# Layer-1 products started on half of the modulation, and its query and key products cut into 256-column matmuls

## The reference, cut to what matters

```
mod = silu(c) @ w_ada + b_ada                 # w_ada: 2048 x 6144, 50 MB
shift, scale, gate = split(mod, 3)
h = rms_norm(x, norm_gain) * (1 + scale) + shift
proj = h @ w_in                               # w_in: 2048 x 8192, 67 MB
q_sb, k_sb, v_sb, z_sb, q_r, k_r, v_r, z_r = split(proj, 8)
... stick-breaking attention on (q_sb, k_sb, v_sb), gated by silu(z_sb)
... chunkwise retention on (q_r, k_r, v_r), gated by silu(z_r)
x = x + gate * (concat(oa, ob) @ w_out)
```

## Time and profile before

| what | value |
|---|---|
| runs shown | 1885.12 us median of 3 (1883.63 to 1887.93) |
| the profiled execution, its own time | 1890.45 us |
| its span, first to last instruction | 1888.6 us |
| TensorE busy, share of the span | 94% |
| VectorE, ScalarE, GpSimd | 65%, 48%, 4% |
| moved from HBM | 346.87 MB |
| mean granted TensorE clock | 0.976 of full speed |

### The profile page before, as it was taken

The page is one execution under the profiler, slowest core; times in us unless marked ns, Lnnn a source line. Parts: engine busy times, 40 slices in busy tenths (PEclk is TensorE's granted clock), DMA queues, the critical chain, the costliest instruction groups (busy, mean ns, idle before and its releaser), DMA issues.

```text
span 1888.6 us, 23572 instructions
## 1 busy us (share of the span) xinstructions
PE 1784.2 (94%) x9703; PEld 1517.6 (80%) x9703; DVE 1235.9 (65%) x1520; ACT 902.7 (48%) x1158; POOL 75.7 (4%) x87
## 2 busy tenths in 40 slices
PE   1699999999999989999999999999989999999897
PEld 1577888888887878888888888788878888878786
DVE  3978767655477655788567766865464667566754
ACT  2333544454356434666344565644354555455632
POOL 0111000000000000011000000000000000000010
PEclk9798999999999999999999999999989999999999
DMA  8897888556444546666654555565546565444463
GB/s 304 328 350 294 296 290 298 153 148 177 135 145 141 190 149 169 188 189 180 178 145 138 153 167 162 167 191 185 187 141 178 162 194 146 123 123 123 134 187 115
DMA packets 304874, 350.51 MB, mean 186 GB/s; under 512 B 10416, under 2 KB 286000, under 8 KB 298624
## 3 DMA queue, kind: packets, MB, share of 16 engines
q1 hardware_dynamic: 297744, 298.34, 52.5%
q0 software_dynamic: 7024, 50.66, 6.9%
HBM read 346.87 MB, written 2.10 MB: 185 GB/s over the span
## 4 chain that ended last, share of the span: by engine, by line
PE 90%; DVE 5%; DMA 2%; ACT 2%; issue 2%; SPq 0%; DVEq 0%
PE psG L431 48%; PE psG L432 24%; PE psG L425 3%; PE psG L426 3%; PE psG L427 3%; DVE ada_sum L1062 1%; DMA P<-in_memT 1%; PE psH L1615 1%; DMA raw<-in_mem_w 1%; PE psH L1604 1%; DVE w_lo L368 1%; PE psH L1629 1%; DVE W L1003 1%; ACT w_hi L364 1%; PE psH L1890 1%
## 5 line engine op out<-in xcount | busy, mean ns | idle before, releaser
L431 PE MATMUL psG<-xA,w_hi 128*128 128x512 f32 x3520 | 1281.8, 407 | 53.4 <-issue 24.4
L432 PE MATMUL psG<-xA,w_lo 128*128 128x256 f32 x3520 | 994.7, 283 | 0.0
L368 DVE TENSOR_TENSOR w_lo<-raw,w_hi 128x1024 fp32r<-128x1024 f32 (+1 forms) x560 | 686.5, 1239 | 356.9 <-ACT w_hi L364 355.4
L431 PEld LDWEIGHTS psG<-xA,w_hi 128*128 128x128 f32 x3520 | 670.0, 190 | 226.5 <-issue 50.1
L364 ACT ACTIVATE w_hi<-raw 128x1024 fp32r<-128x1024 f32 (+1 forms) x560 | 572.9, 1045 | 372.2 <-DMA raw<-in_w_out 163.9
L432 PEld LDWEIGHTS psG<-xA,w_lo 128*128 128x128 f32 x3520 | 673.7, 191 | 4.4 <-issue 3.8
L400 ACT ACTIVATE P<-psG 128x512 f32<-128x512 f32 x102 | 60.6, 594 | 217.5 <-PE psG L432 217.4
L1033 DVE TENSOR_TENSOR P<-psG,P 128x512 f32<-128x512 f32 (+2 forms) x103 | 70.4, 683 | 116.4 <-ACT P L400 114.1
L1062 DVE SCALAR_TENSOR_TENSOR ada_sum<-ada_ring,silc,ada_sum 128x2048 f32<-128x2048 f32 x48 | 112.6, 2347 | 3.9 <-DMA ada_ring<-in_w_ada 3.8
L425 PE MATMUL psG<-w_hi,xA 128*128 128x512 f32 x192 | 77.7, 405 | 4.4 <-DVE memkv L1033 3.9
L426 PE MATMUL psG<-w_lo,xA 128*128 128x512 f32 x192 | 76.9, 400 | 0.0
(11 more groups left out here) (291 smaller groups left out, 1492.0 us busy)
## 6 DMA issues: line engine op xcount, KB each, us to landing
raw<-in_w_in SPq DMA_DIRECT2D x360, 512.0 KB, 3.8
raw<-in_w_out SPq DMA_DIRECT2D x128, 512.0 KB, 3.4
ada_ring<-in_w_ada POOLq DMA_DIRECT2D x48, 1024.0 KB, 7.9
raw<-in_mem_w SPq DMA_DIRECT2D x32, 512.0 KB, 9.3
raw<-in_w_uq SPq DMA_DIRECT2D x24, 384.0 KB, 3.3
raw<-in_w_ukv SPq DMA_DIRECT2D x32, 128.0 KB, 2.4
raw<-in_w_ukv SPq DMA_DIRECT2D x16, 256.0 KB, 3.2
P<-in_memT SPq DMA_DIRECT2D x1, 2048.0 KB, 25.6
```

What stands on the lines that cost most here:

```text
L368: nc.vector.tensor_tensor(slot(w_lo, n), slot(raw, n), slot(w_hi, n), ALU.subtract).then_inc(lo_ready, 1)
L431: nc.tensor.matmul(psG[:, bank + f, :], hi[:, w], x, start=first, stop=False)
L432: last = nc.tensor.matmul(psG[:, bank + f, S:2 * S], lo[:, w], x[:, 0:S], start=False, stop=end)
```

## The change

It has three parts (1 to 3), and a fourth that they bring with them.

1. Modulation in two column halves. The order of `w_ada` is now: columns 0 to 1023 of shift and scale (32 loads of 512 KB), then columns 1024 to 2047 of both (32 loads). The ring has six buffers of 512 KB. The first half is added during `G_MEM` (one per unit, two in each of the first four), then half of the columns of the modulation are summed, and eight of the 16 tiles of the norm are made, in the hooks of the last three units. GpSimd issues its first `w_ada` load after it has helped with the memory's sum of squares (`add_squares(0)`, new), and stops at the 21st for `add_squares(1)`.
2. Layer-1 products split along the rows. `G_SBQK0`, `G_RTQK0`, `G_SBV0` (16, 16 and 8 units) multiply the rows 0 to 1023 of their weights by the tiles of the first half, and ScalarE copies the result to SBUF. During them the second half of the modulation is added, and the other eight tiles are made in the last three units. `G_SBQK`, `G_SBV`, `G_RTQK` (16, 8 and 16 units now) do the rows 1024 to 2047, and VectorE adds their result from PSUM. A block of the four query and key products now has two units instead of four. Half of the `sb_hook` work moves to `G_RTV`.
3. These four query and key products use three matmuls of 256 columns per block of weights (high by high, high by low, low by high) into one half of a bank, so that one engine alone takes the result.
4. The 16 gate loads of 1 MB by GpSimd become 32 of 512 KB that SP issues into the same six `raw` slots as the weights, one after every second weight chunk in `G_SBQK`, `G_SBV`, `G_RTV`, `G_SBZ`, one after every fourth in `G_RTQK` (`GATE_AT`). A slot with a gate chunk is free again when VectorE has added it. The memory is loaded in four pieces ahead of the constants, `x` after the first eight weight chunks.

```diff
-ADA_SLOTS = 4
-ADA_FIRST, ADA_BLOCK = 8, 6
+ADA_SUM, ADA_RING, GATE_SUM = 64, (48, 52, 56, 60, 72, 76), 60
+ADA_HALF = 32
+MEM_UNITS, EARLY_UNITS = 32, 40
...
+        G_SBQK0, G_SBQK = (Gemm(8, 8, columns(w_in, 0, row0=k0 * NP), dst=into(SBQ), pair=True, **early(k0), **one_half) for k0 in (0, 8))
+        G_RTQK0, G_RTQK = (Gemm(8, 8, columns(w_in, 4096, row0=k0 * NP), dst=into(RTQ), **early(k0), **one_half) for k0 in (0, 8))
+        G_SBV0, G_SBV = (Gemm(8, 2, columns(w_in, 2048, 512, 2, row0=k0 * NP), cols=512, kk=2, tokens=copy_tokens(SBV),
+                              **early(k0)) for k0 in (0, 8))
...
+        ORDER = [*G_MEM, G_SBQK0, G_RTQK0, G_SBV0, G_SBQK, G_SBV, G_RTQK, G_RTV, G_SBZ, G_RTZ, G_OUT,
...
+        GATE_AT = {G_SBQK: lambda i: i % 2 == 1, G_SBV: lambda i: i % 2 == 1, G_RTQK: lambda i: i % 4 == 3,
+                   G_RTV: lambda i: i % 2 == 1, G_SBZ: lambda i: i % 2 == 1}
+        ITEMS = []
+        for g in ORDER:
+            for i in range(len(g.order)):
+                ITEMS.append(("weight", g.c0 + i))
+                if g in GATE_AT and GATE_AT[g](i):
+                    ITEMS.append(("gate", sum(kind == "gate" for kind, _ in ITEMS)))
...
+            for j in range(j, end):
+                kind, n = ITEMS[j]
+                if j >= SLOTS:
+                    before, m = ITEMS[j - SLOTS]
+                    sp.wait_ge(*((chunk_used, m + 1) if before == "weight" else (ada_used, 2 * ADA_HALF + m + 1)))
+                if kind == "gate":
+                    k, half = m_to_gate(n)
+                    sp.dma_start(raw[:, j % SLOTS, :], ada_rows(k, 2, half)).then_inc(raw_loaded[j % SLOTS], 16)
+                    continue
...
+                            if g.halves == 1:
+                                out = psG[:, bank + f, 0:S]
+                                nc.tensor.matmul(out, hi[:, w], x[:, 0:S], start=first, stop=False)
+                                nc.tensor.matmul(out, hi[:, w], x[:, S:2 * S], start=False, stop=False)
+                                last = nc.tensor.matmul(out, lo[:, w], x[:, 0:S], start=False, stop=end)
+                                continue
...
             sp.dma_start(vec[:, :], io["vec"]).then_inc(loaded["vec"], 16)
+            for g in range(4):
+                sp.dma_start(mem_raw[:, 4 * g:4 * g + 4, :], io["memT"].rearrange("(t p) s -> p t s", p=NP)[:, 4 * g:4 * g + 4, :])\
+                  .then_inc(mem_loaded[g], 16)
             sp.dma_start(con[:, :], io["con"]).then_inc(loaded["con"], 16)
...
                 load_weights(sp, g)
+                if g is G_MEM[0]:
+                    sp.dma_start(xT[:, :, :], io["xT"].rearrange("(t p) s -> p t s", p=NP)).then_inc(loaded["x"], 16)
...
+            add_squares(0)
+            for m, (half, k, part) in enumerate(ADA_ORDER):
+                slot = m % len(ADA_RING)
+                if m == 20:
+                    add_squares(1)
+                if m >= len(ADA_RING):
+                    pool.wait_ge(ada_used, m + 1 - len(ADA_RING))
+                pool.dma_start(ada_ring[slot][:, :], ada_rows(k, part, half)).then_inc(ada_loaded[slot], 16)
...
+            def gate_hook(g, u0=0):
+                def hook(b, p):
+                    i = 8 * b + p // 2
+                    if p % 2 and GATE_AT[g](i):
+                        ada_add(2 * ADA_HALF + ITEMS[PLACE["weight", g.c0 + i] + 1][1])
+                return hook
...
+            run(G_SBQK, gate_hook(G_SBQK))
+            run(G_SBV, gate_hook(G_SBV))
...
             run_products(pe, G_RTQK, sb_hook)
-            run_products(pe, G_RTV)
+            pe.wait_ge(q["sb_y"], 2)
+            gate_columns(0)
+            run_products(pe, G_RTV, lambda b, p: sb_hook(2 + b, p))
             pe.wait_ge(q["sb_y"], 4)
-            pe.wait_ge(ada_used, 3 * KT)
-            ada_columns(1, 2 * KT, "gate_cols")
...
             run_products(pe, G_SBZ, rt_hook)
+            pe.wait_ge(q["rt_y"], 2)
+            gate_columns(1)
             run_products(pe, G_RTZ, lambda b, p: rt_hook(2 + b, p))
```

More of the change, by code:

```diff
@@ L268, in build, with early @@
         h1 = dict(x=from_a, ready=norm_ready(1))
+        def early(k0):
+            return dict(x=lambda k: xA[:, k0 + k, :], ready=lambda tiles: (q["nm_lo"], 16 + k0 + tiles), adds=k0 > 0, per=8)
+        one_half = dict(halves=1)
         w_in, mem_w = io["w_in"], io["mem_w"]
@@ L445, in build @@
         sb_v, rt_v = (tiles(t, 8).rearrange("p (h f) -> p h f", h=2) for t in (SBV, RTV))
[L446 to L447 removed]
+        ADA_ORDER = [(half, k, part) for half in range(2) for k in range(KT) for part in range(2)]
         GATED1 = [(SBQ, SBZ), (SBQ + 4, SBZ + 4), (RTQ, RTZ), (RTQ + 4, RTZ + 4)]
@@ L679, in _ @@
             run(G_RTQK, sb_hook)
-            run(G_RTV)
             act.wait_ge(loaded["con1"], 16)
+            run(G_RTV, lambda b, p: sb_hook(2 + b, p))
             def rt_hook(n, p):
@@ new lines, in half_norm, with ada_units @@
+            def half_norm(half, step):
+                if step == 0:
+                    modulation(half)
+                    dve.wait_ge(q["nm_rs"], 2)
+                for t in (range(0, 4), range(4, 7), range(7, 10))[step]:
+                    norm_step(1, xT, gs, mod, 8 * half + t, 8 * half, 8 * half + 8)
+            def ada_units(units):
+                done = [0]
+                for u in range(units):
+                    done.append(done[-1] + (u < units - 4) + (units == MEM_UNITS and u < 4) - (units == EARLY_UNITS and u % 9 == 8))
+                return done
@@ new lines, in ada_hook @@
+            def ada_hook(u0, units, half):
+                done = ada_units(units)
+                def hook(b, p):
+                    if p % 2 == 0:
+                        u = u0 + 8 * b + p // 2
+                        for m in range(done[u], done[u + 1]):
+                            ada_add(ADA_HALF * half + m)
+                        if u >= units - 3:
+                            half_norm(half, u - (units - 3))
+                return hook
+            for i, g in enumerate(G_MEM):
+                run(g, ada_hook(8 * i, MEM_UNITS, 0), hook_first=False)
@@ L1142, in sb_hook, with both, hook @@
                     v.tensor_scalar(tiles(n * 2 + SBQ, 2), psH[:, BB, :], 1.0, None, ALU.mult).then_inc(q["sb_y"], 1)
-            run(G_RTQK, sb_hook)
-            run(G_RTV)
-            dve.wait_ge(q["gate_cols"], 1)
-            link(v.tensor_tensor(mod[:, 32:48], psH[:, BD, 32:48], V("b_ada", 32, 16), ALU.add))
+            def both(*hooks):
+                def hook(b, p):
+                    for h in hooks:
+                        h(b, p)
+                return hook
+            run(G_RTQK, both(sb_hook, gate_hook(G_RTQK)))
+            gate_columns(0)
+            run(G_RTV, both(lambda b, p: sb_hook(2 + b, p), gate_hook(G_RTV)))
             sin2 = C1("sin", S).unsqueeze(1).broadcast_to([NP, 2, S])
@@ L1200, in z1_hook @@
                     gate_1(n - 1)
-            run(G_SBZ, z1_hook)
+            run(G_SBZ, both(z1_hook, gate_hook(G_SBZ)))
+            gate_columns(1)
             run(G_RTZ, lambda b, p: z1_hook(2 + b, p))
@@ L1624, in sums_hook, with ada_columns @@
                 return hook
-            def ada_columns(part, column, name, first=True, last=True):
-                for t in range(KT):
-                    ins = mm(psH[:, BD, column + t:column + t + 1], ada_sum[:, part, t * NP:t * NP + NP],
-                             ones[:, 0:1], start=first and t == 0, stop=last and t == KT - 1)
-                ins.then_inc(q[name], 1)
+            def ada_columns(src, column, name, first=True):
+                for t in range(8):
+                    ins = mm(psH[:, BD, column + t:column + t + 1], src[:, t * NP:t * NP + NP], ones[:, 0:1],
+                             start=first and t == 0, stop=bool(name) and t == 7)
+                if name:
+                    ins.then_inc(q[name], 1)
```

342 lines of the change are left out of this document (185 added, 157 removed).

## The result

The changed kernel takes 1969.13 us (median; 1960.5 to 1972.39), the kernel before 1886.53 beside it: a ratio of 1.0428, interval 1.0386 to 1.0471. That is 83 us slower where 8 were forecast, and outside the range of 1852 to 1925. The profiled execution's span is 1970.5 us.

What follows compares the result with a forecast made beforehand. TensorE, busy 94% of 1888.6 us, was taken as the bound. Terms before the gates summed to -47, gates +55, together +8: 1893 us against the median of 1885.12; 8-in-10 range 1852 to 1925, the forecast's own 1880 to 1912.

Steps and rivals of the forecast that it cites:

- Three matmuls of 256 columns: Layer's query and key products: 512 pairs become triples at 0.350 us for 0.353; 0 to -1.5 us, taken as 0.
- Start-up: Before the first product: root at 18.5 us instead of 38.1, first product at 27.8; -21.8 us (-15 to -24).
- The units of `G_MEM`: The 32 units of the memory stage take 106.3 us for 127.9; -21.6 us.
- up to the old pace: Early half-units after `G_MEM`: 10.2 us of serial norm go, 3.7 for columns and 3 for 40 units charged; -3.5 us.
- The cost of `x` in one load: In `G_MEM`: `x` queued behind the eighth chunk makes the ninth come late; +5 us (0 to 10).
- The gate chunks: From `G_SBQK` to `G_RTZ`: gate loads in the weights' slots make TensorE wait for weights; +55 us (30 to 76).
- SP's order closes a circle: Gate stages: addition frees a slot, but waits behind the split of a weight queued behind that slot; 8.2 us per two units.
- the circle's landing: Link in the gate stages' cycle: a load lands in 3.4 us plus 0.8 behind the gate chunk's own data.
- one gate in four units: In `G_RTQK`: gates this far apart close no such cycle; +2 us.
- a clock that drops in the gaps: Gate stages: TensorE's lower clock in its pauses is mostly absorbed by them; no size given.
- the first: Rival, gate stages: cycle hidden, landing near 3.4 us, lead never used up; 1868 or 1838 us; chances 0.20 and 0.13.
- The early part bound by DMA: Second rival, through the early units: 76 MB to load, 20 us of the gain lost, 1913 us; chance 0.12.

Runs made afterwards that it cites:

- a4_pairs: Changed kernel with the layer's queries and keys again by a 512-column and a 256-column product into a whole bank, row split kept; 1968.1 us.
- a1_no_gates: Changed kernel without gate chunk loads, their additions and the gate's column sums, the gate being its bias alone; 1852.7 us, 0.9814 of the kernel before.
- a3_small_gates: Changed kernel with each gate load cut to 32 of 1024 columns, additions, slots, waits and order unchanged; 1944.6 us, 1.0319 of the kernel before.
- a2_add_first: Changed kernel with VectorE's gate addition ahead of its unit's split instead of behind it; 1906.0 us, 1.0107 of the kernel before.
- d1_empty_slots: Changed kernel without gate loads, additions and column sums, but each gate chunk's slot kept empty for its turn; 1891.0 us, 1.0008 of the kernel before.
- b3_both: Changed kernel with gate chunks on GpSimd's queue into three own buffers and two sums, additions moved, and xT in four pieces; 1853.6 us, 0.9821 of the kernel before.

## Why the prediction was wrong

**Three matmuls of 256 columns: right.** Twelve matmuls in the changed kernel's timeline, a weight load for each:

```profile
395.73 0.28 PE L481 MATMUL psG<-xA,w_hi 128*128 128x256 f32 x1
...
397.17 0.28 PE L481 MATMUL psG<-xA,w_hi 128*128 128x256 f32 x1
```

That is 0.120 each, 0.360 for three, against 0.353 for a pair: 3.6 us in 512, where 0 was taken. By the Trainium skill's rule on weight loads (TensorE: Matmul & The Clock Gate, Part 3, what overlaps and what doesn't) it would have been 55 us; the spacing and `a4_pairs` are against it. The same part of the Trainium skill also lets a load into the background weight buffer be pulled ahead of running matmuls, and with that the spacing agrees.

**Start-up: right in size.** The first product is at 30.68 us, not 27.8. From root to product it is the forecast's 9.3; the root is 2.9 later. The chain that ended last, of the changed kernel, shows with what:

```profile
3.31 7.99 DMA con<-in_con
11.35 1.23 PE psH L1730 x2
...
15.92 4.65 PE psH L1730 x10
...
30.68 0.79 PE psG L485
```

TensorE's sums need the ones that are part of the constants. These land at 11.3, not 10.6, and ten sums in a row follow. This row also bears on two experiments: the activations aren't what the first sum waits for, so their pieces gain little; and with six loads of `w_ada` beside them the constants' 7.99 us become 15.40.

```profile
3.58 15.40 DMA con<-in_con
```

So 7.7 of the 19 us gained at the first product come from the issues of `w_ada` that were put off, as forecast. Which edits bring the other 11 wasn't tried one by one.

**The units of `G_MEM`, and up to the old pace.** 115.1 us were measured, 106.3 forecast. The cost of `x` in one load, +5, was of the right kind: with pieces it is 109.8. The forty early half-units take 119.2 us, and the forecast's 253 - 134 is 119. The sum of these parts was to be -47, and `a1_no_gates` has -35 by the ratio (-37.7 by the spans), some 5 of them the column sums that it lacks; 12 us of lateness at 265 are those of the start, 2.9, and of `G_MEM`, 8.8.

**The gate chunks: the step that failed.** It was +55 (30 to 76) and is +116 by `a1_no_gates`, some 111 without the column sums. The forecast was right that SP's order closes a circle and wrong in two ways.

First, the circle's landing was sized too small. The 3.4 us of the earlier trace rows are the landing of weights of `w_out`; those of `w_in`, which are meant here, have a median of 3.8 in the same page, and 0.8 was allowed for the gate chunk's bytes, which cost 1.4 (`a3_small_gates`). That makes the shown turn 9.2 us, and the mean turn is 9.7; which link adds the last 0.5 was not read. Nine turns at 9.7 in place of 8.2, each for two units that need 5.7, are 36 us in place of 23 (an estimate from these rows), and `G_SBQK` and `G_SBV` lose 36.5 (22.5 and 14.0).

Second, and larger, what a short lead does to hooks was left out. The forecast charged 2 in `G_RTQK`, and 8, 20 and 2 in `G_RTV`, `G_SBZ` and `G_RTZ`, where TensorE was taken to wait for weights (for hooks reached late it had 1.5 us in a group of `G_SBZ`). The stages show what the gates cost and what it goes with (us; the order is the changed kernel less `a2_add_first`, the lead `d1_empty_slots` less `a1_no_gates`, the rest `a2_add_first` less `d1_empty_slots`):

| stage | forecast | measured | order | lead | rest |
|---|---|---|---|---|---|
| `G_SBQK`, `G_SBV` | 23 | 36.5 | 33.1 | 1.6 | 1.8 |
| `G_RTQK` | 2 | 15.2 | 8.8 | 1.7 | 4.7 |
| `G_RTV` | 8 | 24.8 | 6.1 | 18.0 | 0.7 |
| `G_SBZ` | 20 | 40.2 | 19.7 | 15.5 | 5.0 |
| `G_RTZ` | 2 | 1.9 | 0.2 | 1.6 | 0.1 |

In `G_RTV` and `G_SBZ` the order costs what the forecast charged for the circle, 25.8 for 28. What it lacked there is the lead, 33.5 us. The split that VectorE waits for is that of a unit three ahead, which TensorE doesn't need yet, and behind it stands the hook work that TensorE needs now. `d1_empty_slots` shows 37 us of this without any circle. In `G_RTQK` the lead costs little. There the forecast was wrong that one gate in four units closes no circle worth counting: 8.8 us hang on the order; by which waits was not read. The rest of 4.7 and 5.0 stands in the stages that end with the gate's column sums.

By the experiments the 116 us are: the order of addition and split 61, the shorter lead 37, bytes some 10, additions and the gate's column sums some 8. The order was changed first and the lead then, and the two can overlap: the 61 are what the order costs while the lead is short.

The forecast also said that a clock that drops in the gaps is mostly absorbed by them. No run holds the clock, so this stays open; of the 34 us that the empty slots cost in `G_RTV` and `G_SBZ`, 11 are TensorE's longer busy time at the lower clock.

Of the rivals, the first is out for the changed kernel, whose turns are 9.7 us. Its 1852 to 1880 holds the 1858.2 of the kernel with buffers of its own, but that one has no circle to hide. The early part bound by DMA is not seen: with `b3_both` the 32 triple units take 2.88 us each, at the matmuls' own spacing.

With `xT` in pieces (`b3_both`) `G_MEM` takes 108.5 us, where the forecast without its +5 would have 101.3. The trace shows where most of these 7 us are: TensorE is busy for 100.0 us, where the forecast's terms for work make 99.3, but it is idle for 8.6, where the forecast had 2. It waits 3.3 us at the first token product for an addition into `memkv`, 2.9 in the sums of squares for GpSimd, and 2.3 for split weights.

## What to carry to other kernels

Before a load is put into another one's ring, write down for each slot who frees it and what stands ahead of that instruction on its engine: if that is work on a load behind the slot, it is a closed circle, and its period is the sum of its links. Count the ring's depth in units of the stage afterwards; when the lead falls to the distance at which an engine works ahead, that engine waits for data that nobody needs yet, with work behind it that somebody needs now. Here the gate chunks cost 6 us with another queue, three buffers and a second sum of their own, where in the shared ring they cost 116.

## What the runs showed of the hardware

A load lands later behind another one's bytes. With 512 KB of a gate chunk issued 0.4 us ahead of it a weight of 512 KB landed after 5.2 us in the changed kernel; with 16 KB in the chunk's place it took 3.8 (`a3_small_gates`), as much as the median of the weights of `w_in` in the kernel before. The 512 KB of constants took 7.99 us behind 2 MB of their own queue, and 15.40 with 3 MB of another queue's beside them.

Matmuls of 256 columns, each with a weight load of its own of 128 x 128, followed each other every 0.120 us.

Pauses of TensorE went with a lower granted clock: 0.89 in the mean of 265 to 624 us in the changed kernel, where it idles for 78 us, against 1.00 in the same stages of `a1_no_gates`, where it idles for 2.
